# Low weight parts of the DeltaNet heads: GpSimd's subtraction replaced by a negated high part and an accumulating transfer

## The chip, the cores and the metric

One core of one Trainium2 chip runs the whole program. The metric is the device time in microseconds (us) of that core for one execution; of several executions the median counts.

## The reference, cut to what matters

The program is a decoder trunk of two layers on 1024 tokens with 1024 channels, all in float32. Each layer normalises its input, multiplies it with one wide projection, runs two token mixers side by side (retention, and a gated DeltaNet in chunks) and merges them.

```
h = rmsnorm(x, norm_g)
proj = h @ w_in                       # 1024 x 9232, float32
(rq, rk, rv, rz, dq, dk, dv, dz, db, da, gr, gd) = split(proj)
o_r = retention(rope(rq), rope(rk), rv), normalised, * silu(rz)
dq, dk, dv = silu(causal_conv([dq, dk, dv]))
o_d = gated_deltanet(l2norm(dq), l2norm(dk), dv, sigmoid(db), g), normalised, * silu(dz)
y = sigmoid(gr) * (o_r @ w_up_r) + sigmoid(gd) * (o_d @ w_up_d)
x = x + y @ w_o
```

## The kernel before, in words

**Products.** A product of float32 matrices is made of three float32r products: the left and right operand are each split into a high part (the value rounded to float32r) and a low part (the value less its high part), and high x high, low x high and high x low are added in PSUM. The activations lie split in `act_hi` and `act_lo`. The weights are taken in blocks of 128 columns: a block is 128 partitions x 8 x 128 floats, 512 KB.

**The way of a weight block.** SP loads it from HBM into `w_raw`, of which there is one (`load_w`). A high part goes to `w_hi`, a low part to `w_lo`, each with two slots that alternate by the block's number g. In the DeltaNet heads ACT writes the high part (`split_hi`, L1429) and GpSimd (POOL in the profile) the low part, `w_raw - w_hi` (`split_w`, L2579). In the rest of the program VectorE or ACT and GpSimd do it. `load_w` waits until the low part of the block before is done, since that frees `w_raw`. PE's `dense_pieces` (L866, L868, L870: the three products) waits for the same signal of its own block, `w_lo_ready`. Splitting block g waits until PE has finished block g - 2, whose slot it takes, so it starts about when PE starts block g - 1.

**Units.** A DeltaNet head is worked in two units, "even" and "odd", one for each half of the 1024 tokens. A unit has 24 slots. PE executes in each slot two pieces of the dense blocks (six matmuls of 512 columns), and between them the small matmuls of the head: the state scan (`ks`, `xu`, `so` for four chunks of 128 tokens, slots 0 to 11), the inverse of the triangular matrix (`solve` on VectorE, then three levels), transposes. A unit covers three weight blocks; their successors' splits stand in slots 0, 8 and 16. The order of every engine is written by `unit_schedule`; each engine goes through the same list in order, and waits on semaphores where the others have to be ready. For the change these places matter:

- ACT, slot 0: evacuation of a dense bank (L1419), `split_hi` (L1429), then the first copy of the state scan from PSUM (`vn`, L1620), for which PE's `so` (L1195) waits.
- ACT, slots 8 and 16: `split_hi` behind an evacuation.
- GpSimd: `split_w` thrice a unit; a small power (L2666) before the one of slot 16; `q` times decay (L2672) after the one of slot 0; two masks (L2659, L2661) after the one of slot 8.
- SP: after the load of one block (`load_w`, L655) come eight stores of the small diagonal blocks to HBM (L725, `l_store`) and two loads of them, spread over partitions (L733, `l_load`). VectorE's triangular solve (L2280 and L2283, 15 steps) needs these. SP's queue is worked in order, so what stands behind a waiting `load_w` waits too.

Units "even" and "odd" run for heads 1 to 7 of each layer: 28 units, with 84 blocks. Between the split of slot 16 and that of slot 0 of the next unit lies the shortest time. The profile's rows name the lines of the kernel as printed here.

Of the kernel before, what the change touches and what calls it, by code (L numbers as in the profile page):

```python
# [28 lines left out]
DH = 8  # L29
# [51 lines left out]
class Signal:  # L81
# [3 lines left out]
    def __init__(self, handle, per):  # L85
        self.sem, self.per = handle, per

    def after(self, t, k):

        return t * self.per + (self.per + k)  # L90
# [206 lines left out]
def build(nc, x, norm_gain, w_in, conv_w, a_log, dt_bias, dn_gain, w_up_ret, w_up_dn, w_out, final_gain,  # L297
          masks, rope, ret, out):
    ctx = ExitStack()
    with ctx:  # L300
# [226 lines left out]
        w_hi_ok, w_lo_ok = signal("w_hi_ready", 1), signal("w_lo_ready", 1)  # L527
# [13 lines left out]
        b_tokps = signal("ba_tokens_psum", 1)  # L541
        b_dve, b_act = signal("ba_vector", 8), signal("ba_scalar", 9)
        b_gcps, b_rowps, b_rows = signal("gc_psum", 1), signal("rows_psum", 1), signal("rows_ready", 2)
# [78 lines left out]

        def v_weights(h):

            return v_later if h else v_first
# [16 lines left out]
        def _(eng):  # L642
# [199 lines left out]
        def _(eng):  # L842
# [514 lines left out]
        def _(eng):  # L1357
# [53 lines left out]
            for l in range(DEPTH):  # L1411
# [12 lines left out]
                def split_hi(g, slot):  # L1424

                    eng.wait_ge(w_in_ok.sem, w_in_ok.after(g, 16))
                    eng.wait_ge(dense_ok[1].sem, dense_ok[1].after(g, -1))
                    eng.wait_ge(w_hi_ok.sem, w_hi_ok.after(g, 0))
                    eng.activation(w_hi[:, slot, :, :], w_raw[:, :, :], ACT.Copy).then_inc(w_hi_ok.sem, 1)  # L1429

# [59 lines left out]
                def delta_unit(kind, h):  # L1490
# [11 lines left out]
                    for step in unit_schedule(kind):  # L1502
# [50 lines left out]
                        elif what == "split" and (kind in ("even", "odd") or kind == "first" and step[1]):  # L1553
                            idx = g0 + step[1] + 1
                            split_hi(g + idx, idx % 2)
# [221 lines left out]
        def _(eng):  # L1777
# [3 lines left out]
            def split_w(g, slot, held=True, second=None):  # L1781


                if second is None:
                    eng.wait_ge(w_in_ok.sem, w_in_ok.after(g, 16))
                else:
                    eng.wait_ge(w2_in.sem, w2_in.after(second, 16))
                    eng.sem_inc(w_in_ok.sem, 16)
                if held:
                    eng.wait_ge(dense_ok[1].sem, dense_ok[1].after(g, -1))  # L1790
                eng.tensor_copy(w_hi[:, slot, :, :], w_from[second is not None][:, :, :]).then_inc(w_hi_ok.sem, 1)

            def low_w(g, slot):

                eng.wait_ge(w_hi_ok.sem, w_hi_ok.after(g, 1))
# [4 lines left out]
            def split_v(l, h, j):  # L1800
# [11 lines left out]
                eng.tensor_copy(hi[:, :, col], w_raw[:, :, :]).then_inc(w_hi_ok.sem, 1)  # L1812
                if h == 0 and j == 1:
                    eng.wait_ge(w_hi_ok.sem, w_hi_ok.after(g, 1))
# [4 lines left out]
            def split_gates(g, held=True):  # L1819
# [4 lines left out]
                eng.tensor_copy(w_hi[:, BLK_BA % 2, :, 0:16], w_raw[:, :, 0:16]).then_inc(w_hi_ok.sem, 2)  # L1824
# [123 lines left out]
            for l in range(DEPTH):  # L1948
# [395 lines left out]
                def ret_head(h, last):  # L2344
# [12 lines left out]
                    for hf in range(NHALF):  # L2357
# [71 lines left out]
                        else:  # L2429
                            g, slot = n + BLK_UPD + 1, (BLK_UPD + 1) % 2  # L2430
                            eng.wait_ge(w_hi_ok.sem, w_hi_ok.after(g, 1))
# [143 lines left out]
        def _(eng):  # L2575
            def split_w(g, slot, second=False):

                eng.wait_ge(w_hi_ok.sem, w_hi_ok.after(g, 1))
                eng.tensor_tensor(w_lo[:, slot, :, :], w_from[second][:, :, :], w_hi[:, slot, :, :].bitcast(F32), ALU.subtract)\  # L2579
                   .then_inc(w_lo_ok.sem, 1)  # L2580

            def split_v(l, h, j):
# [3 lines left out]
                eng.wait_ge(w_hi_ok.sem, w_hi_ok.after(l * NBLK + BLK_RET + 6 * h + 2 + j, 1))  # L2586
# [3 lines left out]
            def split_gates(g):  # L2590

                eng.wait_ge(w_hi_ok.sem, w_hi_ok.after(g, 2))
# [36 lines left out]
            for l in range(DEPTH):  # L2629
# [4 lines left out]
                def delta_unit(kind, h):  # L2634
# [141 lines left out]
```

## Time and profile before

| | |
|---|---|
| time, median of 2 runs | 2645.55 us (2644.49 to 2646.61) |
| span of the profiled execution | 2644.2 us |
| PE busy | 2620.6 us (99%) |
| VectorE (DVE) busy | 1761.1 us (67%) |
| ScalarE (ACT) busy | 704.5 us (27%) |
| GpSimd (POOL) busy | 798.6 us (30%) |
| granted TensorE clock, mean | 0.999 |
| moved by DMA | 217.79 MB, mean 82 GB/s |

The span is the time from the first to the last instruction of one execution; the median of the runs is 1.35 us longer. Busy shares are of the span. PE's matmuls are pipelined, so a busy PE says that matmuls follow one another without a gap, not that each is at its peak.

### The profile page before, as it was taken

How to read it: one execution, taken by the hardware profiler on the slowest of the kernel's cores; microseconds unless marked ns; L12 is line 12 of the kernel's file. 1: busy time of each engine (PE TensorE's matmuls, PEld its weight loads, DVE VectorE, ACT ScalarE, POOL GpSimd, SP SyncE). 2: the span in 40 equal slices, each digit the busy share in tenths (PEclk: the TensorE clock that was granted, in tenths of full speed). 3: DMA queues.
4: the chain of work that ended last, by engine and by line, in shares of the span. 5: the costliest groups of instructions: out<-in, count | busy, mean ns of one | idle time of the engine just before them, and what ended most of it. 6: DMA issues, size and time to landing. Idle time of an engine off the chain costs nothing.

```text
span 2644.2 us, 40210 instructions
## 1 busy us (share of the span) xinstructions
PE 2620.6 (99%) x14874; PEld 2238.1 (85%) x14874; DVE 1761.1 (67%) x3972; ACT 704.5 (27%) x1440; POOL 798.6 (30%) x451
## 2 busy tenths in 40 slices
PE   8999999999999999999999999999999999999998
PEld 6888888888888899888877888888888998898887
DVE  7878777877755555434577778777877555653333
ACT  5333333333311212200143333333332221231001
POOL 3123333333312212334512233332322122132453
PEclk9999999999999999999999999999999999999999
DMA  5321222122211112433533222222222111133344
GB/s 174 100 85 58 81 69 85 53 86 65 85 50 43 41 35 76 130 96 120 157 90 88 77 74 69 73 77 72 67 77 73 43 51 43 41 106 100 99 135 152
DMA packets 293416, 217.79 MB, mean 82 GB/s; under 512 B 31747, under 2 KB 246101, under 8 KB 292965
## 3 DMA queue, kind: packets, MB, share of 16 engines
q1 hardware_dynamic: 259620, 159.07, 20.9%
q10 hardware_dynamic: 33600, 56.15, 6.3%
q8 instruction: 119, 1.95, 0.3%
q14 instruction: 77, 0.62, 0.1%
HBM read 176.30 MB, written 38.86 MB: 81 GB/s over the span
## 4 chain that ended last, share of the span: by engine, by line
PE 92%; DVE 3%; DMA 2%; issue 1%; ACT 1%; SPq 0%; POOL 0%; ACTq 0%; DVEq 0%; POOLq 0%
PE dense_ps L866 23%; PE dense_ps L870 23%; PE dense_ps L868 23%; PE work L849 3%; PE dense_ps L890 2%; PE dense_ps L891 2%; PE dense_ps L892 2%; PE work L1145 1%; PE work L1182 1%; PE work L1202 1%; PE work L1121 1%; PE work L1104 1%; PE work L1171 1%; PE work L1195 1%; PE work L1156 1%
## 5 line engine op out<-in xcount | busy, mean ns | idle before, releaser
L866 PE MATMUL dense_ps<-act_hi,w_hi 128*128 128x512 f32 x2552 | 1048.3, 411 | 1.7 <-DVE w_lo L1797 0.8
L870 PE MATMUL dense_ps<-act_hi,w_lo 128*128 128x512 f32 x2552 | 998.4, 391 | 0.0
L868 PE MATMUL dense_ps<-act_lo,w_hi 128*128 128x512 f32 x2552 | 997.3, 391 | 0.0
L2579 POOL TENSOR_TENSOR w_lo<-w_raw,w_hi 128x1024 fp32r<-128x1024 f32 x162 | 400.1, 2470 | 1024.5 <-ACT w_hi L1429 582.7
L870 PEld LDWEIGHTS dense_ps<-act_hi,w_lo 128*128 128x128 f32 x2552 | 479.0, 188 | 105.8
L866 PEld LDWEIGHTS dense_ps<-act_hi,w_hi 128*128 128x128 f32 x2552 | 481.0, 188 | 86.9 <-POOL act_lo L2600 2.3
L868 PEld LDWEIGHTS dense_ps<-act_lo,w_hi 128*128 128x128 f32 x2552 | 481.5, 189 | 78.8 <-issue 0.5
L1973 DVE SCALAR_TENSOR_TENSOR arena<-arena,cols 128x512 f32<-128x512 f32 x288 | 244.3, 848 | 6.1
L1429 ACT ACTIVATE w_hi<-w_raw 128x1024 fp32r<-128x1024 f32 x94 | 99.1, 1054 | 330.5 <-PE dense_ps L870 310.5
L1419 ACT ACTIVATE arena<-dense_ps 128x512 f32<-128x512 f32 x96 | 57.2, 596 | 258.5 <-PE dense_ps L870 258.5
L849 PE MATMUL work<-mk,arena 128*128 128x128 f32 x768 | 112.1, 275 | 7.9 <-DMA arena<-in_x 7.9
L2280 DVE TENSOR_TENSOR arena<-arena 128x60 f32<-128x60 f32 (+14 forms) x480 | 99.9, 208 | 20.2 <-DMA arena<-l_scratch 7.8
L892 PE MATMUL dense_ps<-v_later_lo,act_hi 128*128 128x256 f32 x384 | 107.9, 281 | 0.0
L890 PE MATMUL dense_ps<-v_later_hi,act_hi 128*128 128x256 f32 x384 | 107.9, 281 | 0.0
L891 PE MATMUL dense_ps<-v_later_hi,act_lo 128*128 128x256 f32 x384 | 107.9, 281 | 0.0
L849 PEld LDWEIGHTS work<-mk,arena 128*128 128x128 f32 x768 | 91.8, 142 | 17.7 <-issue 5.2
L2283 DVE TENSOR_TENSOR arena<-arena 128x60 f32<-128x60 f32 (+14 forms) x480 | 92.4, 192 | 16.5
L2666 POOL TENSOR_TENSOR arena<-arena,negh 128x4 f32<-128x4 f32 x32 | 33.0, 1032 | 230.1 <-DVE arena L2180 230.1
L866 PE MATMUL dense_ps<-o_hi,w_hi 128*128 128x512 f32 x256 | 99.6, 389 | 0.0
L868 PE MATMUL dense_ps<-o_lo,w_hi 128*128 128x512 f32 x256 | 99.6, 389 | 0.0
L870 PE MATMUL dense_ps<-o_hi,w_lo 128*128 128x512 f32 x256 | 99.6, 389 | 0.0
L1620 ACT ACTIVATE arena<-work 128x128 f32<-128x128 f32 x128 | 34.9, 273 | 229.7 <-PE work L1182 224.4
(262 smaller groups left out, 4094.7 us busy)
## 6 DMA issues: line engine op xcount, KB each, us to landing
w_raw<-in_w_in SPq DMA_DIRECT2D x138, 512.0 KB, 3.8
arena<-l_scratch SPq DMA_DIRECT2D x64, 256.0 KB
arena<-gate_scratch ACTq DMA_DIRECT2D x64, 256.0 KB, 2.7
gate_scratch<-arena ACTq DMA_DIRECT2D x36, 256.0 KB, 2.0
w_raw<-in_w_out SPq DMA_DIRECT2D x18, 512.0 KB, 3.7
o_scratch<-arena ACTq DMA_DIRECT2D x32, 256.0 KB, 2.2
w_raw<-in_w_up_dn SPq DMA_DIRECT2D x16, 512.0 KB, 3.6
arena<-o_scratch ACTq DMA_DIRECT2D x32, 256.0 KB, 3.7
```

What stands on the lines that cost most here:

```text
L849: mm = eng.transpose(wk[bank][:, c * P:(c + 1) * P], src, ident)
L866: eng.matmul(dense_ps[:, to, :], w_hi[:, slot, k, :], hi[:, k, seg], start=(k == 0), stop=False)
L868: eng.matmul(dense_ps[:, to, :], w_hi[:, slot, k, :], lo[:, k, seg], start=False, stop=False)
L870: mm = eng.matmul(dense_ps[:, to, :], w_lo[:, slot, k, :], hi[:, k, seg], start=False, stop=(k == KT - 1))
L890: eng.matmul(dst, act_hi[:, k, tok], hi[:, k, :], start=(k == 0), stop=False)
L891: eng.matmul(dst, act_lo[:, k, tok], hi[:, k, :], start=False, stop=False)
L892: mm = eng.matmul(dst, act_hi[:, k, tok], lo[:, k, :], start=False, stop=(k == KT - 1))
L1429: eng.activation(w_hi[:, slot, :, :], w_raw[:, :, :], ACT.Copy).then_inc(w_hi_ok.sem, 1)
L1973: eng.scalar_tensor_tensor(out=acc[:, i % 2, :], in0=src, scalar=wcol, in1=acc[:, i % 2, :], op0=ALU.mult, op1=ALU.add).then_inc(conv_s.se ...
L2280: eng.tensor_tensor(xm[:, :, 0:left], column, xs[:, :, k:k + 1].to_broadcast([P, CPH, left]), ALU.mult).then_inc(sv_s.sem, 1)
L2283: eng.tensor_tensor(xs[:, :, k + 1:BASE], xs[:, :, k + 1:BASE], xm[:, :, 0:left], ALU.add)\
L2579: eng.tensor_tensor(w_lo[:, slot, :, :], w_from[second][:, :, :], w_hi[:, slot, :, :].bitcast(F32), ALU.subtract)\
```

## The change

In the 84 blocks of the "even" and "odd" units the low part is made in another way. ACT writes the high part as before, and then, in a second activation, its negation into `w_lo` (a copy with scale -1.0, rounded alike). GpSimd, in place of the subtraction, issues a DMA that reads `w_raw` and adds it to `w_lo` in SBUF, so that `w_lo` becomes `w_raw - w_hi`. GpSimd signals `w_lo_ready` right after it has issued the transfer; the landing has two semaphores of its own, for even and odd block numbers (`w_lo_added_even`, `w_lo_added_odd`). Whoever waited for the low part of such a block (PE ahead of the block, and `load_w` of the next block) now waits for both. Since ACT signals twice for a block, `w_hi_ready` counts two a block everywhere. Three semaphores of the start of a layer are merged into one (`Later`) to make room. Nothing else moves.

```diff
@@ signals
-        w_hi_ok, w_lo_ok = signal("w_hi_ready", 1), signal("w_lo_ready", 1)
+        w_hi_ok, w_lo_ok = signal("w_hi_ready", 2), signal("w_lo_ready", 1)
+        w_added = [plain("w_lo_added_even"), plain("w_lo_added_odd")]
...
+        def added(g):
+
+            l, q = g // NBLK, g % NBLK - BLK_HEADS
+            assert 1 <= q <= 6 * (DH - 1)
+            return w_added[g % 2], 16 * len([1 for m in range(l + 1) for i in range(1, 6 * (DH - 1) + 1)
+                                             if m * NBLK + BLK_HEADS + i <= g and (m * NBLK + BLK_HEADS + i - g) % 2 == 0])
@@ SP, load_w
                 eng.wait_ge(w_lo_ok.sem, w_lo_ok.after(g, -ahead))
+                if 1 <= (g - 1) % NBLK - BLK_HEADS <= 6 * (DH - 1):
+                    eng.wait_ge(*added(g - 1))
                 eng.dma_start(w_from[other][:, :, :], src).then_inc((w2_in if other else w_in_ok).sem, 16)
@@ PE, dense_pieces
                                 eng.wait_ge(w_lo_ok.sem, w_lo_ok.after(g, 1))
+                                if 1 <= g % NBLK - BLK_HEADS <= 6 * (DH - 1):
+                                    eng.wait_ge(*added(g))
@@ ACT
+                def split_signed(g, slot):
+
+                    eng.wait_ge(w_in_ok.sem, w_in_ok.after(g, 16))
+                    eng.wait_ge(dense_ok[1].sem, dense_ok[1].after(g, -1))
+                    eng.wait_ge(w_hi_ok.sem, w_hi_ok.after(g, 0))
                     eng.activation(w_hi[:, slot, :, :], w_raw[:, :, :], ACT.Copy).then_inc(w_hi_ok.sem, 1)
+                    eng.activation(w_lo[:, slot, :, :], w_raw[:, :, :], ACT.Copy, scale=-1.0).then_inc(w_hi_ok.sem, 1)
@@ GpSimd
+            def add_w(g, slot):
+
+                eng.wait_ge(w_hi_ok.sem, w_hi_ok.after(g, 2))
+                eng.dma_start(w_lo[:, slot, :, :], w_raw[:, :, :], accum_op=ALU.add)\
+                   .then_inc(w_added[g % 2], 16)
+                eng.sem_inc(w_lo_ok.sem, 1)
...
+                            elif kind in ("even", "odd"):
+                                add_w(g + idx, idx % 2)
                             elif kind != "first" and not is_v(idx):
                                 split_w(g + idx, idx % 2)
```

ACT, from the split of slot 16 of one unit to the first state step of the next (the second piece begins one row later in the same split, at its second activation). L1555 or L1530 is an evacuation to `gate_t`, L1436 or L1419 one to `raw`, L1648 or L1620 the copy `vn`. Before:

```order
L1429 ACTIVATE w_hi<-w_raw 128x1024
L1629 DMA o_scratch<-arena 128x512
L1419 ACTIVATE arena<-dense_ps 128x512
L1435 ACTIVATE arena<-arena 128x512
L1590 ACTIVATE arena<-arena 128x256
L1592 ACTIVATE arena<-arena 128x256
L1435 ACTIVATE arena<-arena 128x512
L1419 ACTIVATE arena<-dense_ps 128x512
L1598 ACTIVATE arena<-mk 128x64
L1429 ACTIVATE w_hi<-w_raw 128x1024
L1620 ACTIVATE arena<-work 128x128
```

And now:

```order
L1454 ACTIVATE w_lo<-w_raw 128x1024
L1657 DMA o_scratch<-arena 128x512
L1436 ACTIVATE arena<-dense_ps 128x512
L1460 ACTIVATE arena<-arena 128x512
L1618 ACTIVATE arena<-arena 128x256
L1620 ACTIVATE arena<-arena 128x256
L1460 ACTIVATE arena<-arena 128x512
L1436 ACTIVATE arena<-dense_ps 128x512
L1626 ACTIVATE arena<-mk 128x64
L1453 ACTIVATE w_hi<-w_raw 128x1024
L1454 ACTIVATE w_lo<-w_raw 128x1024
L1648 ACTIVATE arena<-work 128x128
```

A second activation of 128x1024 stands between `split_hi` and what followed it: a DMA issue and an evacuation in slot 16, the copy `vn` in slot 0.

GpSimd, around the same splits, with the semaphores that each row waits for. Before:

```order
L2676 TENSOR_TENSOR arena<-arena,negh 128x4 [waits o_norm_steps]
L2666 TENSOR_TENSOR arena<-arena,negh 128x4 [waits v_scale,key_scalars]
L2579 TENSOR_TENSOR w_lo<-w_raw,w_hi 128x1024 [waits w_hi_ready] x2
L2672 TENSOR_TENSOR arena<-arena 128x512 [waits o_psum,exp_gc_ready,kqv_ready]
L2579 TENSOR_TENSOR w_lo<-w_raw,w_hi 128x1024 [waits w_hi_ready]
L2659 TENSOR_TENSOR arena<-mk,arena 128x512 [waits level_v_psum,gc_row_loaded]
```

And now:

```order
L2713 TENSOR_TENSOR arena<-arena,negh 128x4 [waits o_norm_steps]
L2703 TENSOR_TENSOR arena<-arena,negh 128x4 [waits v_scale,key_scalars]
L2613 DMA w_lo<-w_raw 128x1024 [waits w_hi_ready] x2
L2709 TENSOR_TENSOR arena<-arena 128x512 [waits o_psum,exp_gc_ready,kqv_ready]
L2613 DMA w_lo<-w_raw 128x1024 [waits w_hi_ready]
L2696 TENSOR_TENSOR arena<-mk,arena 128x512 [waits level_v_psum,gc_row_loaded]
```

The places are the same. The subtraction has become a DMA issue; it waits for the same signal, which now comes after the second activation.

SP, around the same splits, with its waits. Before:

```order
L715 DMA arena<-row_scratch 128x512 [waits exp_gc_ready,masked_gc]
L655 DMA w_raw<-in_w_in 128x8x128 [waits w_lo_ready] x2
L725 DMA l_scratch<-arena 16x4x16 [waits l_blocks_loaded,neg_l_ready]
L725 DMA l_scratch<-arena 16x4x16 x7
L733 DMA arena<-l_scratch 128x1x512 [waits solve_steps,l_blocks_stored]
```

And now:

```order
L670 DMA w_raw<-in_w_in 128x8x128 [waits w_lo_added_odd,w_lo_ready]
L670 DMA w_raw<-in_w_in 128x8x128 [waits w_lo_added_even,w_lo_ready]
L740 DMA l_scratch<-arena 16x4x16 [waits l_blocks_loaded,neg_l_ready]
L740 DMA l_scratch<-arena 16x4x16 x7
L748 DMA arena<-l_scratch 128x1x512 [waits solve_steps,l_blocks_stored]
```

The stores and loads of the diagonal blocks stand, as before, behind a load of weights, which now waits for the landing of the accumulating transfer too.

## Rows read from the trace of the kernel before

**Rows 1.** The page, whole span: busy engines, then PE clock over 40 slices.
```profile
PE 2620.6 (99%) x14874; PEld 2238.1 (85%) x14874; DVE 1761.1 (67%) x3972; ACT 704.5 (27%) x1440; POOL 798.6 (30%) x451
...
PEclk9999999999999999999999999999999999999999
```

**Rows 2.** Busy time by engine in the head stretches of both layers.
```profile
core 0: us, PE busy (x) PEld busy (x) DVE busy (x) ACT busy (x) POOL busy (x), PEclk, DMA share, GB/s
120.00:717.00 597.00, 597.00 (x3521) 509.90 (x3520) 484.11 (x1218) 203.22 (x437) 179.24 (x107) 1.00 0.25 72
1430.00:2025.00 595.00, 595.00 (x3507) 508.23 (x3506) 481.65 (x1212) 201.90 (x435) 179.77 (x107) 1.00 0.25 72
```

**Rows 3.** Waits of PE, whole span: total us, times, longest.
```profile
PE work L1171 <- DVE arena L2314: 2.9, 1, 2.9
```

**Rows 4.** ACT in order of time: start us, us, engine, line, operation.
```profile
306.61 1.05 ACT L1429 ACTIVATE w_hi<-w_raw 128x1024 fp32r<-128x1024 f32 x1
...
318.93 1.04 ACT L1429 ACTIVATE w_hi<-w_raw 128x1024 fp32r<-128x1024 f32 x1
319.87 0.26 ACT L1620 ACTIVATE arena<-work 128x128 f32<-128x128 f32 x1
...
351.68 1.06 ACT L1429 ACTIVATE w_hi<-w_raw 128x1024 fp32r<-128x1024 f32 x1 [0.57 <-ACT arena L1541]
...
363.32 1.04 ACT L1429 ACTIVATE w_hi<-w_raw 128x1024 fp32r<-128x1024 f32 x1
364.27 0.26 ACT L1620 ACTIVATE arena<-work 128x128 f32<-128x128 f32 x1
```

**Rows 5.** POOL in order of time, same stretch.
```profile
352.43 1.01 POOL L2666 TENSOR_TENSOR arena<-arena,negh 128x4 f32<-128x4 f32 x1 [5.71 <-DVE arena L2180]
353.41 2.38 POOL L2579 TENSOR_TENSOR w_lo<-w_raw,w_hi 128x1024 fp32r<-128x1024 f32 x1
364.45 2.40 POOL L2579 TENSOR_TENSOR w_lo<-w_raw,w_hi 128x1024 fp32r<-128x1024 f32 x1 [8.65 <-ACT w_hi L1429]
```

**Rows 6.** SP's queue in order of time.
```profile
355.82 0.38 SPq L655 DMA_DIRECT2D w_raw<-in_w_in  x1
356.30 3.80 SPq L725 DMA_DIRECT2D l_scratch<-arena  x8
361.14 1.21 SPq L733 DMA_DIRECT2D arena<-l_scratch  x2
```

**Rows 7.** PE in order of time: the scan's first state step, two units.
```profile
321.04 0.38 PE L1195 MATMUL work<-arena 128*128 128x128 f32 x2
...
365.19 0.38 PE L1195 MATMUL work<-arena 128*128 128x128 f32 x2
```

**Rows 8.** The page's DMA issues: KB each, median us to landing.
```profile
gate_scratch<-arena ACTq DMA_DIRECT2D x36, 256.0 KB, 2.0
...
arena<-row_scratch SPq DMA_DIRECT2D x30, 256.0 KB, 4.2
...
x_scratch<-o_all SPq DMA_DIRECT2D x1, 4096.0 KB, 11.7
x_scratch<-o_all SPq DMA_DIRECT2D x2, 2048.0 KB, 8.0
```

**Rows 9.** Tile w_raw: its instructions, ns min/median/max, and its transfers' landing.
```profile
L2579 POOL TENSOR_TENSOR w_lo<-w_raw,w_hi x162: 2376/2396/3306, 99.5 to 2622.2; 128x1024 fp32r<-128x1024 f32 x162
...
DMA to landing us min/median/max: 2.1/3.8/8.9
```

**Rows 10.** DVE in order of time.
```profile
353.74 2.34 DVE L1970 TENSOR_SCALAR arena<-arena,cols 128x512 f32<-128x512 f32 x1
...
368.30 0.24 DVE L2280 TENSOR_TENSOR arena<-arena 128x60 f32<-128x60 f32 x1
```

**Rows 11.** DVE line L1970, ns min/median/max, from 140 to 717 us.
```profile
L1970 DVE TENSOR_SCALAR arena<-arena,cols x39: 475/802/2343, 142.0 to 707.7; 128x512 f32<-128x512 f32 x39
```

**Rows 12.** Waits in the first layer's heads, 140 to 717 us.
```profile
DVE arena L2223 <- PE work L1121: 12.5, 13, 1.0
```

More of the change, by code:

```diff
@@ L81, with __init__, Later @@
 class Signal:
-    def __init__(self, handle, per):
-        self.sem, self.per = handle, per
+    def __init__(self, handle, per, before=0):
+        self.sem, self.per, self.count = handle, per, before
     def after(self, t, k):
-        return t * self.per + (self.per + k)
+        return t * self.per + (self.per + self.count + k)
+def Later(first, before):
+    return Signal(first.sem, first.per, first.count + before)
 def constants():
@@ L1428, in split_hi @@
                     eng.wait_ge(w_hi_ok.sem, w_hi_ok.after(g, 0))
+                    eng.activation(w_hi[:, slot, :, :], w_raw[:, :, :], ACT.Copy).then_inc(w_hi_ok.sem, 2)
+                def split_signed(g, slot):
+                    eng.wait_ge(w_in_ok.sem, w_in_ok.after(g, 16))
+                    eng.wait_ge(dense_ok[1].sem, dense_ok[1].after(g, -1))
+                    eng.wait_ge(w_hi_ok.sem, w_hi_ok.after(g, 0))
                     eng.activation(w_hi[:, slot, :, :], w_raw[:, :, :], ACT.Copy).then_inc(w_hi_ok.sem, 1)
+                    eng.activation(w_lo[:, slot, :, :], w_raw[:, :, :], ACT.Copy, scale=-1.0).then_inc(w_hi_ok.sem, 1)
                 def conv_tanh(t, i):
@@ L1554, in delta_unit @@
                             idx = g0 + step[1] + 1
-                            split_hi(g + idx, idx % 2)
+                            if kind == "first":
+                                split_hi(g + idx, idx % 2)
+                            else:
+                                split_signed(g + idx, idx % 2)
                         elif what == "tanh":
@@ L1790, in split_w @@
                     eng.wait_ge(dense_ok[1].sem, dense_ok[1].after(g, -1))
-                eng.tensor_copy(w_hi[:, slot, :, :], w_from[second is not None][:, :, :]).then_inc(w_hi_ok.sem, 1)
+                eng.tensor_copy(w_hi[:, slot, :, :], w_from[second is not None][:, :, :]).then_inc(w_hi_ok.sem, 2)
             def low_w(g, slot):
-                eng.wait_ge(w_hi_ok.sem, w_hi_ok.after(g, 1))
+                eng.wait_ge(w_hi_ok.sem, w_hi_ok.after(g, 2))
                 eng.wait_ge(w_lo_ok.sem, w_lo_ok.after(g, 0))
@@ L1811, in split_v @@
                 col = slice(j * P, (j + 1) * P)
-                eng.tensor_copy(hi[:, :, col], w_raw[:, :, :]).then_inc(w_hi_ok.sem, 1)
+                eng.tensor_copy(hi[:, :, col], w_raw[:, :, :]).then_inc(w_hi_ok.sem, 2)
                 if h == 0 and j == 1:
-                    eng.wait_ge(w_hi_ok.sem, w_hi_ok.after(g, 1))
+                    eng.wait_ge(w_hi_ok.sem, w_hi_ok.after(g, 2))
                     eng.wait_ge(w_lo_ok.sem, w_lo_ok.after(g, 0))
@@ L1823, in split_gates @@
                     eng.wait_ge(dense_ok[1].sem, dense_ok[1].after(g, -1))
-                eng.tensor_copy(w_hi[:, BLK_BA % 2, :, 0:16], w_raw[:, :, 0:16]).then_inc(w_hi_ok.sem, 2)
+                eng.tensor_copy(w_hi[:, BLK_BA % 2, :, 0:16], w_raw[:, :, 0:16]).then_inc(w_hi_ok.sem, 4)
             def norm_mean(t, b):
@@ L2430, in ret_head @@
                             g, slot = n + BLK_UPD + 1, (BLK_UPD + 1) % 2
-                            eng.wait_ge(w_hi_ok.sem, w_hi_ok.after(g, 1))
+                            eng.wait_ge(w_hi_ok.sem, w_hi_ok.after(g, 2))
                             eng.wait_ge(w_lo_ok.sem, w_lo_ok.after(g, 0))
@@ L2585, in split_v @@
                 hi, lo = v_weights(h)
[L2586 removed]
+                eng.wait_ge(w_hi_ok.sem, w_hi_ok.after(l * NBLK + BLK_RET + 6 * h + 2 + j, 2))
                 eng.tensor_tensor(lo[:, :, col], w_raw[:, :, :], hi[:, :, col].bitcast(F32), ALU.subtract)\
@@ L2590, in split_gates @@
             def split_gates(g):
-                eng.wait_ge(w_hi_ok.sem, w_hi_ok.after(g, 2))
+                eng.wait_ge(w_hi_ok.sem, w_hi_ok.after(g, 4))
                 eng.tensor_tensor(w_hi[:, BLK_BA % 2, :, 16:32], w_raw[:, :, 0:16],
```

7 lines of the change are left out of this document (4 added, 3 removed).

## The prediction

> **What bounds the kernel now.** I read the page first. PE is busy 2620.6 of 2644.2 us, at full clock in every slice [rows 1]. The change acts only in the units of heads 1 to 7, so the question is what PE does there. Windows over these stretches of both layers answer it: PE is busy 597.00 of 597.00 us and 595.00 of 595.00 us, while DVE is busy for 81%, ACT for 34% and POOL for 30% [rows 2]. In the list of waits the longest entry of PE outside the start is a single one of 2.9 us [rows 3]. So nothing that gets faster on another engine can shorten the heads; a matmul in line is all that counts. What the change can do is make PE wait. That has to be read from the slack of the weight chain, on the engines' timelines.
>
> **What goes.** Of the 162 subtractions on POOL, 84 go, at a median of 2.396 us [rows 9]: 201 us of POOL. POOL is 30% busy there, so this is worth nothing on the path. A DVE instruction beside it gets shorter: L1970 took 2.34 us when it met the subtraction at 353.41, and takes 0.475 at best [rows 5, 10, 11]. This is worth nothing either, as DVE already waits for PE once in nearly every unit, up to 1.0 us [rows 12].
>
> **What comes on ACT.** One more activation of 128x1024 per block. The row beside it: the next instruction starts 0.94 to 0.95 us after `split_hi` started [rows 4], so each adds 0.95. In slots 8 and 16 nothing urgent stands behind it. In slot 0 the first `vn` does. In the unit that starts at 363.32 (even), `vn` ran from 364.27 for 0.26 us; now it ends at 364.27 + 0.95 + 0.26 = 365.48. A signal from ACT to another engine takes 0.09 us (`split_hi` ends at 364.36, POOL starts at 364.45) [rows 4, 5]. That is 365.57, and PE's L1195 stood at 365.19 [rows 7]: PE waits 0.38. In the unit from 318.93 (odd) the same sum gives 319.87 + 0.95 + 0.26 + 0.09 = 321.17 against 321.04: 0.13. Over 14 units of each kind: 14 x 0.51 = **7.1 us**, certain as far as the rows go.
>
> **What comes on the transfers.** There is one `w_raw`. The loop is: high part, negated part, add, next load, next split. With D for the time from POOL's wait being met to the landing of the add: 0.95 + 1.04 (two activations) + 0.09 + D + 0.03 (SP) + 3.8 (median landing of a load of weights [rows 9]) = 5.9 + D. The time that PE's pace leaves for it is the distance of the splits: 318.93 - 306.61 = 12.3 us into an odd unit, and 363.32 - 351.68 = 11.6 us into an even one [rows 4]. The other splits are further apart (from 318.93 to 351.68 there are two intervals, 16.4 on average). So the load is late from D = 11.64 - 5.9 = 5.7 us on in one interval of a pair, and from 6.4 in the other. A late load holds ACT in slot 0, with `vn` behind it, so PE waits for all of the lateness, on top of the 0.38 or 0.13. POOL's power ahead of slot 16's add (1.01 us from 352.43 [rows 5]) ends before the second activation does, so it adds nothing.
>
> Added time = 14 x (max(0, D - 5.7) + 0.38) + 14 x (max(0, D - 6.4) + 0.13).
>
> **How large is D?** No row shows an accumulating transfer, or any transfer issued by POOL. Nearest rows: a 256 KB store lands after 2.0 us, a 2048 KB one after 8.0, a 4096 KB one after 11.7 [rows 8]. From 256 to 2048 KB that is 3.4 us per MB. The add reads 1 MB (both blocks) and writes 0.5 MB. If the write runs beside the read, 2.0 + 0.75 x 3.4 = 4.6 us; if not, 2.0 + 1.25 x 3.4 = 6.2. POOL has to issue it: its smallest instruction takes 1.01 us [rows 5]. That gives 5.6 to 7.2 us. I take **6.0**, in the lower half, since a read and a write are different directions. Outer bounds: 3.7 from below (a plain load's 3.8, nearly), 8.9 from above (the slowest landing of a 512 KB load [rows 9]).
>
> A rule of the Trainium skill can be set beside this. "DMA: Bandwidth & Descriptors", section "Anatomy of one DMA — SWDGE (gpsimd) path", fits a transfer issued by GpSimd as 2.0 us plus its bytes at 436 GB/s; for the 1 MB read that would be 4.4 us, an estimate. By it the load would never be late, and only the 7.1 us would stay. No row of this trace can show it, and it says nothing of the accumulation.
>
> **Sum at D = 6.0.** 14 x (0.3 + 0.38) + 14 x 0.13 = 9.5 + 1.8 = 11.3 us. The span is 2644.2 us and the median of the runs 1.35 longer, so 2645.55 + 11.3 = **2657 us**, 0.4% more.
>
> **What stands behind SP's wait.** The stores and loads of the diagonal blocks follow the load in SP's queue. They began at 356.30, after a subtraction that ended at 355.79 [rows 5, 6]. Now the add is issued at 351.68 + 2.08 = 353.76 and lands at 359.8; they begin 3.9 us later. The last of the two loads of the blocks went out at about 361.7 and landed, by the 4.2 us of another 256 KB load to all partitions [rows 8], at 365.9; now at 369.8. DVE's solve needs it at 368.30 [rows 10], and at 369.0 when PE waits 0.7 in between. So 0.8 us may be missing. I put this at nothing, because DVE waits for PE inside this stretch (rows 12: once a unit, up to 1.0 us) and catches up there; if it doesn't, 14 x 0.8 = 11 us come on top. With a larger D it does not grow, since PE's own wait moves the need as well.
>
> **Rivals.**
> (a) *All hidden*: D under 5.7. Then 7.1 us: 2653. Speaks for it: the load of 512 KB lands in 3.8. Against: twice the bytes are read, and POOL has to issue.
> (b) *The transfer bounds the loop*: the one mechanism by which the kernel gets slower by 2%. The threshold is 52.9 us = 28 D - 169.4 + 7.1, so D = 7.7. At 8.9 us: 14 x (3.2 + 0.38) + 14 x (2.5 + 0.13) = 87 us: 2733. For it: an accumulation that reads and writes in turn sits at 7.2 already. Against: the DMA engines are used only 25% there [rows 2]. From D = 9 the wider intervals would begin to be late too.
> (c) *POOL is kept from issuing by DVE.* The trace shows that the two engines hold each other up: L1970 lasted 2.34 us, until POOL's subtraction was over, against 0.475 alone [rows 5, 10, 11]. In the other direction the add, due at 353.76, would meet L1970, issued at 353.74, and other DVE work behind it. If that costs one such hold of 1.9 us and a bit (D = 8.5): 14 x (2.8 + 0.38) + 14 x (2.1 + 0.13) = 76 us: 2721. If it costs one undisturbed L1970, 0.5 us, it is in the forecast's range. The Trainium skill states such a rule ("SBUF — State Buffer", section "Who interferes with whom"): a DVE instruction in a two-port mode and GpSimd's making of descriptors exclude each other, for the whole instruction. The trace agrees on the exclusion with a computing POOL; no row shows a transfer issued there.
> (d) *POOL isn't relieved*: issuing takes it as long as the subtraction did. POOL itself has room, but D grows by 1.4 to 7.4: 14 x (1.7 + 0.38) + 14 x (1.0 + 0.13) = 45 us: 2690.
> (e) *A gain.* It would need PE to have a wait that goes. There is none in the heads [rows 2].
>
> **How the numbers follow.** Forecast (D from 5.7 to 7.7): 0.54. (a) 0.17, (d) 0.03; these are within 2%, which is about what a measurement of this kernel can tell from no change: 0.74. (b) 0.14 and (c) 0.10: slower, 0.24. (e) 0.02. The range starts at 2646 (waits of PE smaller than worked out) and reaches to the upper bound of D, 2733; beyond it lies about a third of (b).
>
> **What the profile of the changed kernel would show.** The negated copy: 84 activations of 1.05 us, and L1648 (`vn`) 0.95 later in slot 0. Waits of PE for `vn` at the scan's first `so`, 28 of them: 0.1 to 0.4 us if the load is in time, more where it is late, and then ACT's `split_hi` waits for the DMA of `w_raw` in every second slot 0 first. D itself: from the DMA on POOL's queue to SP's next load. L1970 back at 0.5 us. Splits 8 and 16 without a wait for a load. If PE shows waits at L1141 (the first level), the late diagonal blocks are the cause, and my zero was wrong. If ACT waits for the load in slots 8 and 16 as well, D is over 9 us and the forecast far too low. I would be wrong above all by the size of D.

## The result and the profile after

| | before | after |
|---|---|---|
| time, median of 2 runs each | 2645.55 us | 2704.91 us (2702.17 to 2707.66) |
| span of the profiled execution | 2644.2 us | 2705.8 us |
| granted TensorE clock, mean | 0.999 | 0.995 |

The ratio is 1.0223, with a 95% interval from 1.0193 to 1.0252: 59 us slower, where 11 us were forecast. The time lies inside the range; the likeliest case was far too low.

The page and the windows come first, as in [rows 1] and [rows 2].

```profile
PE 2645.0 (98%) x14874; PEld 2240.8 (83%) x14874; DVE 1719.7 (64%) x3972; ACT 782.9 (29%) x1524; POOL 666.9 (25%) x451
...
PE 68%; DMA 12%; DVE 11%; SPq 4%; issue 3%; POOL 1%; ACT 1%; DVEq 0%; ACTq 0%; POOLq 0%
```

The second of these rows, in the kernel before:

```profile
PE 92%; DVE 3%; DMA 2%; issue 1%; ACT 1%; SPq 0%; POOL 0%; ACTq 0%; DVEq 0%; POOLq 0%
```

The windows of the two head stretches, each moved and lengthened to cover about the same work (the counts of matmuls differ by under 1%):

```profile
120.00:748.00 628.00, 611.46 (x3540) 513.64 (x3540) 463.92 (x1219) 241.53 (x480) 118.88 (x109) 0.99 0.42 103
1462.00:2085.00 623.00, 608.72 (x3538) 511.34 (x3536) 463.07 (x1216) 241.34 (x480) 121.11 (x109) 1.00 0.42 103
```

PE, busy for every microsecond of the heads before, is now idle for 16.5 and 14.3 us of them. The stretches are 31 and 28 us longer; what is not idle time stands in PE's busy time, as matmuls at a lower clock (below) and as the start of each stall, which the modelled ends of the matmuls cover. On the chain that ends last (the second row of the page) DMA and SP's queue have 12% and 4%; before they had 2% and 0%. Note also the granted clock, 0.99 in the first stretch.

What was waited for, over the whole span (us in total, times, longest us):

```profile
DVE arena L2308 <- DMA arena<-l_scratch: 79.0, 31, 5.8
PE work L1188 <- DVE arena L2342: 29.4, 21, 4.3
PEld work L1188 <- issue: 40.6, 29, 4.7
PE work L1212 <- ACT arena L1648: 6.3, 7, 2.3
PEld work L1212 <- ACT arena L1648: 19.2, 30, 2.7
ACT w_hi L1453 <- DMA w_raw<-in_w_in: 0.8, 1, 0.8
```

Three facts stand there. The load of the weights is late for ACT's split once in 84, by 0.8 us. VectorE's triangular solve (L2308, L2280 before) waits for the small diagonal blocks in 31 places. PE waits before `ks` (L1188, L1171 before) for VectorE's state update: 29.4 us by its own rows, and 40.6 us by those of its weight loads (PEld). What is lost lies between the two, as the next rows show.

One even unit in order of time shows how they hang together. It is the place of [rows 4 to 6]; its split of slot 16 starts at 363.15 in place of 351.68. ACT, GpSimd, SP's queue, DVE and PE, each in its own fence:

```profile
363.15 1.06 ACT L1453 ACTIVATE w_hi<-w_raw 128x1024 fp32r<-128x1024 f32 x1 [0.55 <-ACT arena L1566]
...
364.12 1.04 ACT L1454 ACTIVATE w_lo<-w_raw 128x1024 fp32r<-128x1024 f32 x1
```

```profile
365.46 0.92 POOL L2613 DMA_DIRECT2D w_lo<-w_raw  x1 [0.53 <-ACT w_lo L1454]
```

```profile
370.11 0.38 SPq L670 DMA_DIRECT2D w_raw<-in_w_in  x1
370.58 3.81 SPq L740 DMA_DIRECT2D l_scratch<-arena  x8
375.44 1.21 SPq L748 DMA_DIRECT2D arena<-l_scratch  x2
```

```profile
382.52 0.27 DVE L2308 TENSOR_TENSOR arena<-arena 128x60 f32<-128x60 f32 x1 [2.38 <-DMA arena<-l_scratch]
...
385.60 0.35 DVE L2342 SCALAR_TENSOR_TENSOR arena<-arena,work 128x128 f32<-128x128 f32 x1
```

```profile
383.03 0.38 PE L1212 MATMUL work<-arena 128*128 128x128 f32 x2
...
386.09 0.46 PE L1188 MATMUL work<-arena 128*128 128x128 f32 x2 [0.85 <-DVE arena L2342]
```

From the start of the split to the loads of the blocks it is now 375.44 - 363.15 = 12.29 us; it was 361.14 - 351.68 = 9.46 [rows 4, 6]. The blocks are 2.83 us later. The solve starts 382.52 - 363.15 = 19.37 us after the split, before 368.30 - 351.68 = 16.62 [rows 4, 10]: 2.75 us later. The landing is 382.52 - 375.44 = 7.08 us after the first of the two loads began to be issued. If it took as long before, the blocks were there at 361.14 + 7.08 = 368.22, against a need at 368.30: the slack was 2.83 - 2.75 = 0.08 us. VectorE works in order: the state update L2342 stands behind six steps of the solve, although PE's L1212, whose result it takes, was done at 383.41. So PE waits 0.85 us at 386.09 by its row. The matmul before began at 384.86, and without a stall the next begins 0.23 us later, so 1.00 us are lost there; the weight loads' row has 1.25.

This unit is an ordinary one. Leaving out the first solve of each layer, VectorE waited for the blocks 29 times. In 24 of these they landed 6.4 to 7.7 us after the first load began, and in the other five, all among the six longest waits, 8.6 to 10.0 us; the median of the 29 is 7.1. In the kernel before, from the third solve of each layer on, those of the even units start 6.8 to 7.3 us after that load, so their slack was small throughout, and those of the odd units 8.1 to 8.3 us in 12 of 14, about 1.2 us more.

### The profile page after: what moved, and what is told of

Read it like the earlier page. It is cut to its first block, busy times and chain, and to the rows that moved or that the text cites. A ratio compares the mean times of both kernels' runs of the same rounds, so it can differ in the third digit from the quotient of the medians.

```text
span 2705.8 us, 40483 instructions
## 1 busy us (share of the span) xinstructions
PE 2645.0 (98%) x14874; PEld 2240.8 (83%) x14874; DVE 1719.7 (64%) x3972; ACT 782.9 (29%) x1524; POOL 666.9 (25%) x451
## 4 chain that ended last, share of the span: by engine, by line
PE 68%; DMA 12%; DVE 11%; SPq 4%; issue 3%; POOL 1%; ACT 1%; DVEq 0%; ACTq 0%; POOLq 0%
PE dense_ps L883 16%; PE dense_ps L887 16%; PE dense_ps L885 16%; DMA arena<-l_scratch 6%; DMA w_lo<-w_raw 4%; SPq L740 3%; PE dense_ps L907 2%; PE dense_ps L908 2%; PE dense_ps L909 2%; PE work L864 2%; DVE arena L2308 2%; DMA l_scratch<-arena 1%; DVE arena L1998 1%; DVE arena L2311 1%; PE work L1162 1%
## 5 line engine op out<-in xcount | busy, mean ns | idle before, releaser
L2607 POOL TENSOR_TENSOR w_lo<-w_raw,w_hi 128x1024 fp32r<-128x1024 f32 x78 | 198.5, 2544 | 457.1 <-DVE w_hi L1819 450.5
L2613 POOL DMA_DIRECT2D w_lo<-w_raw x84 | 78.9, 939 | 732.2 <-ACT w_lo L1454 720.7
L2001 DVE SCALAR_TENSOR_TENSOR arena<-arena,cols 128x512 f32<-128x512 f32 x288 | 229.4, 797 | 6.1
L2308 DVE TENSOR_TENSOR arena<-arena 128x60 f32<-128x60 f32 (+14 forms) x480 | 99.8, 208 | 91.3 <-DMA arena<-l_scratch 79.0
L1436 ACT ACTIVATE arena<-dense_ps 128x512 f32<-128x512 f32 x96 | 57.2, 596 | 241.8 <-PE dense_ps L887 241.8
L1648 ACT ACTIVATE arena<-work 128x128 f32<-128x128 f32 x128 | 34.8, 272 | 244.9 <-PE work L1199 240.0
L2311 DVE TENSOR_TENSOR arena<-arena 128x60 f32<-128x60 f32 (+14 forms) x480 | 92.5, 193 | 16.5
L1446 ACT ACTIVATE w_hi<-w_raw 128x1024 fp32r<-128x1024 f32 x10 | 10.6, 1061 | 316.3 <-PE dense_ps L887 310.2
```

The source lines that it names most:

```text
L2001: eng.scalar_tensor_tensor(out=acc[:, i % 2, :], in0=src, scalar=wcol, in1=acc[:, i % 2, :], op0=ALU.mult, op1=ALU.add).then_inc(conv_s.se ...
L2308: eng.tensor_tensor(xm[:, :, 0:left], column, xs[:, :, k:k + 1].to_broadcast([P, CPH, left]), ALU.mult).then_inc(sv_s.sem, 1)
L2311: eng.tensor_tensor(xs[:, :, k + 1:BASE], xs[:, :, k + 1:BASE], xm[:, :, 0:left], ALU.add)\
```

## The experiments

Each kernel was timed in 3 rounds beside the kernel before (median 2643.98 to 2645.43 us there), e11_mask_first in 5. Theory Q: the late diagonal blocks in SP's queue, plus the late `vn` copy. Theory A: ScalarE's second activation. Theory T: the transfer, by its traffic or by its hold on GpSimd and VectorE. The table's first row is from the 2 runs each of the change and of the kernel before.

| kernel | time, us | ratio to before (95% interval) |
|---|---|---|
| the change | 2704.91 | 1.0223 (1.0193 to 1.0252) |
| e1_neg_only | 2672.09 | 1.0101 (1.0086 to 1.0116) |
| e7_release_3us_later | 2809.75 | 1.0616 (1.0598 to 1.0633) |
| e3_plain_copy | 2663.43 | 1.0071 (1.0056 to 1.0086) |
| e2_blocks_stored_first | 2664.1 | 1.0076 (1.0061 to 1.0091) |
| e4_vn_before_negation | 2696.12 | 1.0195 (1.0175 to 1.0215) |
| e5_before_stored_first | 2643.57 | 1.0001 (0.9992 to 1.0011) |
| e6_both_mended | 2652.85 | 1.0030 (1.0018 to 1.0042) |
| e8_load_paused | 2658.39 | 1.0057 (1.0040 to 1.0074) |
| e12_load_paused_twice | 2695.88 | 1.0197 (1.0181 to 1.0212) |
| e9_neg_only_stored_first | 2675.58 | 1.0121 (1.0106 to 1.0136) |
| e10_neg_only_both | 2670.19 | 1.0099 (1.0082 to 1.0116) |
| e11_mask_first | 2669.51 | 1.0087 (1.0070 to 1.0104) |

### The blocks taken out from behind the load

```diff
@@ SP, unit_loads, in the changed kernel
+                    l_store(2 * h + 2, 0)
                     load_w(m + BLK_HEADS + 4, w_src(l, w_in, GD0 + P + h * P))
-                    l_blocks(2 * h + 2, 0)
+                    l_load(2 * h + 2)
```

The same is done for the odd blocks (`2 * h + 3`).

> The changed kernel with SP's queue in another order: the eight stores of the diagonal blocks ahead of the load of weights that they followed, the two loads of them still behind it. Theory Q: the two loads go out about 3 us earlier and the solve starts on time; only the 7 us of the first state copy and a few outliers stay: 2650 to 2665. Theory A: about 2700. Theory T: about 2700.

Measured: 2664.1, as theory Q had it; 41 us of the 59 are gone (39 by the two ratios, each taken beside the kernel before), though the transfer, its waits and the second activation are all there (its landing is 4.8 us). The stores no longer stand behind the wait (SP's queue, the same place of this kernel):

```profile
357.86 4.73 SPq L740 DMA_DIRECT2D l_scratch<-arena  x8
362.89 0.39 SPq L670 DMA_DIRECT2D w_raw<-in_w_in  x1
363.80 1.22 SPq L748 DMA_DIRECT2D arena<-l_scratch  x2
```

At this place the two loads begin 363.80 - 355.67 = 8.13 us after the split of slot 16, which is 1.33 us sooner than in the kernel before. So the edit takes away more than the lateness: a landing that the transfer's traffic makes longer is covered by it too. VectorE's waits for the blocks shrink from 79.0 us in 31 places to this:

```profile
DVE arena L2311 <- DMA arena<-l_scratch: 2.8, 2, 1.6
```

The control, the same edit in the kernel before:

> The kernel before, with SyncE's stores of the diagonal blocks issued before the weight load that they stood behind (as in e2_blocks_stored_first). Control for that experiment: if the order is a gain by itself, it does not measure what the change costs. Theory Q: the stage's slack for these blocks was 0.1 us in the even unit and not negative, so nothing to gain: 2641 to 2647. Theories A and T say the same. If it comes out below 2635, the gain in e2_blocks_stored_first was in part one that the kernel before could have had too.

2643.57 against 2643.98: nothing. So the order is no gain by itself, and the 41 us are a cost of the change.

### The `vn` copy

```diff
@@ ACT, slot 0: the negated copy goes behind the first vn
                     eng.activation(w_hi[:, slot, :, :], w_raw[:, :, :], ACT.Copy).then_inc(w_hi_ok.sem, 1)
+                    if not later:
+                        negated(slot)
...
+                            if c == 0 and kind in ("even", "odd"):
+                                negated((g0 + 1) % 2)
```

> The changed kernel, with ScalarE's negated copy of slot 0 moved behind the first `vn` copy of that slot; the transfer of that block then starts later by about one `vn` copy (0.6 to 0.8 us), and nothing else moves. Theory Q (most of the 59 us is the late diagonal blocks, the rest the second activation): the waits of PE for `vn` go, the waits of DVE for l_scratch stay; 2690 to 2702, so 3 to 15 us less than the changed kernel. Theory A (the second activation on ScalarE is the main cost): 2650 to 2675. Theory T (the transfer itself, by its traffic): 2700 to 2710.

> The changed kernel with both: the diagonal blocks stored before the load, and slot 0's `vn` copy ahead of the negated activation. Theory Q: what is left is the later arrival of the low parts at TensorE and slot 8; 2646 to 2658. Theory A: 2645 to 2655 too, but then e4_vn_before_negation is low by itself as well. Theory T: above 2690.

2696.12 and 2652.85: 9 us less without, and 11 us less with, the other mend. Both came out as Q said, but only the second is clear of noise: the intervals of the change (1.0193 to 1.0252) and of e4_vn_before_negation (1.0175 to 1.0215) overlap. What is left of the change after both is 2652.85 - 2643.98 = 9 us.

### A delay with nothing else of the change

GpSimd's subtraction and one activation, as before; only SP's loads come later, by one or two tiny transfers that it waits for.

```diff
@@ SP, load_w, in the kernel before (range(2) in e12_load_paused_twice)
                 eng.wait_ge(w_lo_ok.sem, w_lo_ok.after(g, -ahead))
+                if 1 <= (g - 1) % NBLK - BLK_HEADS <= 6 * (DH - 1):
+                    paused[0] += 16
+                    eng.dma_start(pause[:, :], masks[0:8, 0:P]).then_inc(w_added[0], 16)
+                    eng.wait_ge(w_added[0], paused[0])
                 eng.dma_start(w_from[other][:, :, :], src).then_inc((w2_in if other else w_in_ok).sem, 16)
```

> The kernel before (GpSimd's subtraction, one activation, no accumulating transfer), where SyncE, ahead of each weight load that the change makes later, sends 4 KB from DRAM to DRAM and waits for it. Only the loads and what is queued behind them come later, by the landing of a small transfer, some 2 us. Theory Q: two such pauses stand ahead of each unit's diagonal blocks, of which only the last one before them is fully additive; with a slack of 0.1 us in the even and 1.2 us in the odd unit, DVE waits for l_scratch 1.5 to 2.5 us more in the even and 0.5 to 1.5 in the odd: 2670 to 2695. Theories A and T: there is no second activation and no such traffic, so 2643 to 2650.

> e8_load_paused with two small transfers, each waited for, ahead of each of the 84 loads: 3.7 us of pause, about as late as the change makes these loads (3.9 us by the rows of one even unit). Theory Q: DVE's waits for l_scratch as in the changed kernel, about 80 us in 30 waits, even and odd units, and 36 to 50 us of time: 2680 to 2695, with no transfer on GpSimd's queue and no second activation. Theories A and T: as the kernel before or as e8_load_paused, 2645 to 2660.

One pause measured 1.85 us (from 356.78 to the load at 358.63) and cost 14 us, under the range that I gave: the odd units, for which I had put 0.5 to 1.5 us each, had almost no wait at all. Two pauses took 4.05 us (365.64 to 369.69 in SP's queue) and cost 52 us, 0.9 us over the range; one pause lay above the 2643 to 2650 of theories A and T, and two far above their 2645 to 2660. DVE's waits, of e8_load_paused and then of e12_load_paused_twice:

```profile
DVE arena L2310 <- DMA arena<-l_scratch: 32.0, 18, 3.6
```

```profile
DVE arena L2311 <- DMA arena<-l_scratch: 75.5, 30, 5.0
PE work L1192 <- DVE arena L2345: 32.6, 26, 3.4
```

The second looks like the changed kernel (79.0 in 31, and 29.4 in 21), with no second activation and no accumulating transfer. So lateness of the load, with what is queued behind it, is enough by itself for tens of microseconds. The cost is not in proportion: the first 1.85 us cost 14, the next 2.2 cost 37; the number of VectorE's waits rises from 18 to 30, as the odd units, which have more slack, join in.

The match is not exact, though. Two pauses delay the loads of the blocks by 4.1 us against the split, where the change delays them by 2.83, since the 3.9 us of the prediction, which they were made to copy, was too much. In return the blocks land sooner in that kernel: 5.7 to 7.2 us after the first load began, 6.0 in the median of 28 waits, never 8.6 or more. An estimate by a straight line between the two pauses (delays of 1.8 and 4.1 us, costs of 14 and 52) gives 31 us for a delay of 2.83. The other 10 of the 41 us would then go with the later landing of the blocks beside the accumulating transfer, which is theory T in part. No run tried that by itself.

An earlier attempt at the same question was a poor instrument. GpSimd there does more subtraction before it frees `w_raw`:

```diff
@@ GpSimd, in the kernel before
+                for ks in (slice(0, 2), slice(0, KT)):
+                    eng.tensor_tensor(w_lo[:, slot, ks, :], w_raw[:, ks, :], w_hi[:, slot, ks, :].bitcast(F32), ALU.subtract)
...
```

> The kernel before with one thing added: in the 84 blocks GpSimd runs the subtraction over a quarter of the block and over the whole block once more ahead of the real one, so that w_raw is released some 3 us later, as in the changed kernel, with no second activation and no transfer. Theory Q: most of the 59 us, 2680 to 2705. Theory A and theory T: 2645 to 2650, since PE reads the low part some 10 us later only.

It cost 165 us, far over every expectation. The added GpSimd work also moves the masks and holds VectorE, whose busy time rose to 1922.5 us from 1761.1 [rows 1], so it separates nothing.

### The transfer without the accumulation

```diff
-                eng.dma_start(w_lo[:, slot, :, :], w_raw[:, :, :], accum_op=ALU.add)\
+                eng.dma_start(w_lo[:, slot, :, :], w_raw[:, :, :])\
```

In this kernel the low part holds the raw block, not the difference.

> The changed kernel with a plain transfer from w_raw to w_lo in place of the accumulating one (the low part then holds the raw block, so the sum is another one). It reads 0.5 MB less. If the second read costs 1.2 us of the landing's 5.1, theory Q gives 28 x 1 us less at most: 2675 to 2695, and 2705 if the landing does not change. Theory A: 2705. Theory T: about 2685, as a third of the traffic is gone.

The page's DMA issues, of the changed kernel and then of this one (KB each, median us to landing):

```profile
w_lo<-w_raw POOLq DMA_DIRECT2D x84, 512.0 KB, 5.1
```

```profile
w_lo<-w_raw POOLq DMA_DIRECT2D x84, 512.0 KB, 3.1
```

It lands 2.0 us sooner, and the time is 2663.43, lower than Q's 2675: 41 us less. VectorE still waits for the blocks, but only 24.8 us in 19 places. This cannot tell lateness from traffic, since a plain copy also reads less; the pauses show only what lateness can do alone. It does show that 2.0 us of landing, in this range, are worth as much as taking the blocks out of the queue.

### The second activation with the subtraction

```diff
@@ GpSimd, in the changed kernel, with the waits on the transfer's landing taken out
-                eng.dma_start(w_lo[:, slot, :, :], w_raw[:, :, :], accum_op=ALU.add)\
-                   .then_inc(w_added[g % 2], 16)
-                eng.sem_inc(w_lo_ok.sem, 1)
+                eng.tensor_tensor(w_lo[:, slot, :, :], w_raw[:, :, :], w_hi[:, slot, :, :].bitcast(F32), ALU.subtract)\
+                   .then_inc(w_lo_ok.sem, 1)
```

> The changed kernel with GpSimd's subtraction put back in the 84 blocks: the second activation stays, the transfer and its waits are gone. Theory Q (the diagonal blocks' transfers stand in SP's queue behind the load of weights, which is released later; VectorE's solve starts late and PE waits): the load is released only 0.95 us later than before, so there is the 7 us of PE waiting for the first state copy and a few us of late solves: 2652 to 2662 us. Theory A (the second activation on ScalarE is what costs): about 2705. Theory T (the transfer's traffic slows the other transfers): about 2653.

> e1_neg_only (ScalarE's second activation kept, GpSimd's subtraction back, no transfer) with the diagonal blocks stored before the load. In e1_neg_only DVE hardly waited for l_scratch, so theory Q gives little: the 28 us of e1_neg_only are then ScalarE's second activation (late `vn` copies) and the subtraction that begins 1.05 us later and meets other VectorE work: 2665 to 2672. If instead the blocks, 1.05 us later against a slack of 0.1, are a part of it: 2650 to 2662.

> The same with slot 0's `vn` copy ahead of the negated activation too: e6_both_mended with GpSimd's subtraction where that has the transfer. Theory Q: it differs from e6_both_mended (2652.9) by what the transfer spares DVE and POOL against the subtraction. If sparing the subtraction is worth anything on the path, this is above 2656; if it is worth nothing, 2650 to 2654. The late `vn` copies cost 11 us between e2_blocks_stored_first and e6_both_mended, so this should be 8 to 13 below e9_neg_only_stored_first.

2672.09, 2675.58 and 2670.19. The first is 10 us over Q's range and 19 over T's figure. Storing the blocks first did not lower it (it came 4 us over the range for that), so they have no part in it. Moving `vn` took 5 us, not 8 to 13. Some 26 us stay that no theory had before e1_neg_only was measured. The rows that changed are VectorE's convolution steps, which in e10_neg_only_both took 1052 ns each against 848 before. The costliest groups, of before and then of that kernel (busy us, mean ns):

```profile
L1973 DVE SCALAR_TENSOR_TENSOR arena<-arena,cols 128x512 f32<-128x512 f32 x288 | 244.3, 848 | 6.1
```

```profile
L2007 DVE SCALAR_TENSOR_TENSOR arena<-arena,cols 128x512 f32<-128x512 f32 x288 | 303.0, 1052 | 6.1
```

The subtraction starts one activation later and meets other VectorE instructions; PE then waits for VectorE in the levels and at `xu`. That is what the rows suggest. It was not tried by itself. What e10_neg_only_both does show is a comparison: behind the second activation, GpSimd's subtraction (2670.19) is 17 us dearer than the transfer with its waits (2652.85).

### The 9 us that are left

In e6_both_mended a mask on GpSimd meets a VectorE instruction that it did not meet before. GpSimd and DVE of that kernel:

```profile
339.26 1.59 POOL L2706 TENSOR_TENSOR arena<-mk,arena 128x512 f32<-128x512 f32 x1
340.52 1.55 POOL L2708 TENSOR_TENSOR arena<-arena,mk 128x512 f32<-128x512 f32 x1
```

```profile
339.37 3.00 DVE L2008 TENSOR_SCALAR arena<-arena,cols 128x512 f32<-128x512 f32 x1
```

At the same place of the kernel before:

```profile
337.38 0.80 DVE L1970 TENSOR_SCALAR arena<-arena,cols 128x512 f32<-128x512 f32 x1
```

```diff
@@ GpSimd, in e6_both_mended: the add of slot 8 goes behind the masks
+                                if kind == "even" and step[1] == 1:
+                                    behind_mask = idx
+                                else:
+                                    add_w(g + idx, idx % 2)
...
                             eng.tensor_tensor(dect, gcb3, bcast4(mk[:, C_NT:C_NT + P]), ALU.add).then_inc(m_ok.sem, 1)
+                            if kind == "even":
+                                add_w(g + behind_mask, behind_mask % 2)
```

> e6_both_mended with one step of GpSimd's moved: in the even unit it makes the two masks before it issues the slot's transfer, not after. In e6_both_mended the first mask runs from 339.26 us to 340.85 us and VectorE's TENSOR_SCALAR of the same unit, started at 339.37 us, takes 3.00 us, where the kernel before has 0.80 us at that place. Theory Q with this as what is left of the 9 us: if the masks' inputs are there before ScalarE's copies, the masks run earlier, the TENSOR_SCALAR takes 0.5 to 0.8 us again, and 14 even units give back up to 0.4 us each on TensorE: 2644 to 2650. If the masks' inputs come no sooner, the masks stay where they are and the transfer comes 3 us later: 2652 to 2660.

This missed its target, and the time lies above both of its ranges: the collision at 339.37 is in the odd unit, and the edit moved the even unit's masks. The collision stands there as before (2.99 us, at 342.32 in this kernel), so nothing is learned about it. In the even units the masks came earlier, after this wait of GpSimd, and the transfer behind them at 385.91 in place of 382.96:

```profile
POOL arena L2709 <- DMA arena<-row_scratch: 108.7, 14, 10.0
```

It cost 17 us against e6_both_mended (15 by the ratios); PE now waits in the levels for VectorE's L2328, 10.5 us in 14 places, against 0.6 us once in e6_both_mended.

The rows do say where the 9 us can lie. In e6_both_mended, and in the changed kernel, TensorE's weight loads wait once in every odd unit at a level step for VectorE:

```profile
PEld work L1165 <- DVE arena L2301: 8.9, 15, 0.7
```

```profile
PEld work L1162 <- DVE arena L2291: 8.4, 14, 0.7
```

The kernel before has no such wait at this step (L1145 for L2263), and the two kernels with pauses have 0.6 us in 2 places. At the place shown VectorE's step L2301 starts 4.35 us after the TENSOR_SCALAR that collided, at 343.72, where before it was 2.77 us, and the weight loads wait 0.61 us at 344.19. Matmuls lose 0.35 us there (343.62 to 344.19 is 0.57 us, where 341.62 to 341.84 was 0.22 before), which for 14 odd units is an estimate of 5 of the 9 us. All 14 odd units have both, a TENSOR_SCALAR of 2.65 to 3.06 us and the wait behind it. But no run took the collision away, so it is a candidate and not shown. No version here beats the kernel before.

## Why the prediction was right and wrong

- **What bounds the kernel.** Right. Nothing that was relieved shortened anything: 201 us of GpSimd's subtractions went, its busy time fell by 131.7 us and VectorE's by 41.4, and no time came back.
- **The transfer's D.** Taken as 6.0 us, from 5.6 to 7.2; the landing is 4.5 us at least, 5.1 in the median and 9.5 at most. At the median the loop is 5.9 + 5.1 = 11.0 us, under the 11.6 that the shortest interval leaves. (GpSimd begins to issue 0.30 us after ScalarE is done, 365.16 to 365.46, not 0.09; the landing is counted from the start of the issue.) The load is in time, as the one wait of 0.8 us says. So the 4.2 us that the sum gave to late loads were nothing, and rival (b), the mechanism that I had made the slow case, did not occur. The estimate by the Trainium skill ("DMA: Bandwidth & Descriptors", section "Anatomy of one DMA — SWDGE (gpsimd) path") was 4.4 us for the 1 MB read, 0.7 under the median; for the plain copy of 0.5 MB the same fit gives 3.2, and the trace has 3.1.
- **Rivals (c) and (d).** The issue on GpSimd took 850 ns at least, 878 in the median and 1252 at most, against 2.4 us of the subtraction [rows 9]. VectorE never held it for a whole long instruction. Both fell.
- **The second activation.** `vn` later in slot 0 was priced at 7.1 us. Taken away, it gave 11 us, and 9 that is not clear of noise: the right place, somewhat too small.
- **The step that failed: "I put this at nothing".** It is the paragraph on what stands behind SP's wait. The mechanism was seen, with the queue, the blocks and the solve, and the delay was put at 3.9 us (its own figures give 4.0), which was 2.83, since the transfer landed sooner than supposed. Two terms were wrong. First the landing: I took 4.2 us from another transfer of 256 KB, the load of `row_scratch`, and counted it from the second load, so the blocks seemed to be there at 365.9 with 2.4 us to spare. They land 7.08 us after the first load begins (in the changed kernel), which is 368.22, so the slack was 0.08 us. That they would land later beside the transfer, 7.1 us in the median against 6.0 with two pauses in its place, and five times 8.6 to 10.0, was not in the prediction at all. The trace of before could have told it in part: VectorE waited for these very loads there already, five times:

```profile
DVE arena L2280 <- DMA arena<-l_scratch: 7.8, 5, 4.4
```

- Second, the cover: VectorE's wait for PE once a unit was to absorb it. It doesn't, because VectorE is in order and PE's next state step needs an update that is queued behind the solve. The alternative that I had priced, 11 us, was too low as well; taking the blocks out gives 41. That the time still lies in the stated range is luck: the range was that wide for a late load of weights, which did not occur.
- **The sign that I named.** It was to be PE waiting at the first level. It came one step earlier, at `ks` (L1188), before the level is reached.
- **A term that was missing: the clock.** It is a part of the 41 us. Three windows around the longest wait of the changed kernel (the column before the last two is the granted clock):

```profile
470.00:480.00 10.00, 5.78 (x33) 4.66 (x31) 3.48 (x15) 1.36 (x3) 0.00 (x0) 0.91 0.85 218
480.00:490.00 10.00, 9.96 (x49) 8.73 (x50) 6.68 (x28) 2.88 (x4) 0.17 (x1) 0.75 0.00 1
490.00:500.00 10.00, 10.00 (x65) 8.51 (x65) 9.13 (x21) 4.83 (x14) 4.44 (x4) 1.00 0.48 107
```

PE had waited for 4.26 us, until 480.04. Windows of 1 us show the two levels, full clock and 0.50, which is 1.2 GHz:

```profile
478.00:479.00 1.00, 0.00 (x0) 0.00 (x0) 0.86 (x5) 0.00 (x0) 0.00 (x0) 0.57 1.03 309
480.00:481.00 1.00, 0.96 (x3) 0.93 (x4) 0.83 (x6) 0.00 (x0) 0.00 (x0) 0.50 0.00 0
485.00:486.00 1.00, 1.00 (x7) 0.85 (x6) 0.66 (x2) 0.00 (x0) 0.00 (x0) 1.00 0.00 0
```

Of full clock 3.4 us are missing there in all, but 0.9 of them fell into PE's wait and cost nothing. There are five such places in the heads, each at one of VectorE's six longest waits for the blocks, with nine windows of 10 us at 0.86, 0.97, 0.91, 0.75, 0.88, 0.95, 0.98, 0.85 and 0.83. At the other four the clock fell only when PE was at work again, and took 1.7 us each; at the one shown 2.5 us fell on matmuls. That is some 9 us in all. In e2_blocks_stored_first and e6_both_mended the mean is 0.999, as before. So of the 41 us some 32 are waits, and some 9 are matmuls at the lower clock at the longest of them.

The sum as measured: 41 (blocks, the clock in it) + 11 (`vn`) + 9 (open) = 61 us against 2643.98. By the ratios, each taken beside the kernel before, it is 39 + 12 + 8 = 59 us. The sum closes because each term is the difference of two kernels in a row; it does not prove the terms by itself.

## What to carry to other kernels

Before a wait is put at the head of an in-order queue, list everything that is queued behind it, and take the slack of each from when that very transfer lands and when its user starts, not from another transfer of the same size, and allow for a landing that gets longer beside new traffic. A cover that lies on another in-order engine is no cover if the bound engine needs something that stands behind the late step there. Where the order can be mended, store first and wait later: the same change then costs 0.3% with `vn` moved too, in place of 2.2%.

## What the runs showed of the hardware

- A 512 KB accumulating transfer inside SBUF, issued by GpSimd, landed after 4.5, 5.1 and 9.5 us (least, median, most); the plain one after 3.1 (median). Its issue holds GpSimd for 0.88 us in the median, the plain one's for 0.59.
- Two loads of 256 KB each that spread small blocks over the partitions landed 7.1 us (median of 29) after the first began in the changed kernel, and 6.0 us (median of 28) with two pauses and no accumulating transfer. Issuing the two takes 1.2 us of it. A single load of `row_scratch`, 256 KB too, lands in 4.2 [rows 8].
- SP needs 3.80 us for the eight small stores, but sometimes more: 5.53 us at 461.17 in the changed kernel, where VectorE then waited 5.81 us. Such issues are in the trace of before too (4.58 us at 488.41), where they cost nothing.
- Five of PE's stalls, of 2.1 to 4.3 us, came with a fall of the granted clock to 1.2 GHz, which took another 1.7 us of PE's time at four of them and 2.5 at the fifth. The length of the stall did not decide it: one of 2.12 us (to 1447.20) was followed by a fall, one of 2.77 us (to 1769.82) was not.
